# The mixer's loops in a two-block network: fill slices in one piece, weight parts in quarters, v transposes and the fifth loop moved

## The chip, the cores and the metric

The kernel runs on one core of one Trainium2 chip. Its time is the device time of one execution in microseconds (us); the median of three runs of the kernel before is 1939.12 (1939.05 to 1939.25). One program computes everything: TensorE (PE), VectorE (DVE), ScalarE (ACT), GpSimd (POOL) and SyncE (SP) each run their own queue in order and wait for one another by semaphores.

## The reference, cut to what matters

The input is 512 tokens of 1024 features. A first block is a token mixer and a gated feed-forward network with a short convolution. The second block has two layers, each with three attention branches. The change touches the token mixer alone:

```python
p = einsum('btd,de->bte', xn, w_in)            # 14 panels of weights
gB, gC, hA = split(p[..., :3 * CONV_DIM], 3)
y_a = gC * causal_dwconv(gB * hA, conv_a_w)
r, k, v, wd, ad, gd = split(shifted(p[..., 3 * CONV_DIM:]))
for each token:                                # _wkv7, state S of 64 x 64 for each of 8 heads
    sa = S @ (-kk_t)
    S = S * w_t + sa (kk_t * a_t)^T + v_t k_t^T
    y_t = S @ r_t
y_b = (group_norm(y) + bonus) * gate
out = concat(y_a, y_b) @ w_out
```

Everything is in float32. Each large product is made as three products of rounded parts: high x high, high x low and low x high.

## The kernel before

**Recurrence.** The tokens are taken in 4 tiles of 128 (TT), each of two chunks of 64. For a tile, `scores_0` makes the masked product of the two key forms. The inverse of a triangular 64 x 64 matrix for each head and chunk then comes from 6 levels (LEVELS). A level is: `level` on PE (L954, from the second level on also a transposition, L958), the masked step `T` on DVE (L1844), from the second level on the copy `inverse_t` on ACT (L1403), `update` on PE (L971), and the add into the inverse on DVE (L1853), which the next `level` waits for. These are groups of 32 small matmuls on quarters of the array. `whole_inverse` transposes the result.

**Five loops.** Loop c makes the inverse of tile c and, beside it, the state work of tile c - 1: `turn_bk`, `scores_1`, `scores_23` (L932; DVE masks them, L1829 and L1837), `kav` (L995, two ACT copies, L1419), and for each of the two chunks `state_rhs` (L1007), `state_sa` (L1043) and `state_out` (L1058, L1067, L1075); `values` (L1025, L1028) stands once for a tile. So there is a fifth loop (c = 4) with no inverse. This text calls c = 0 the first loop.

**Fill.** Between the small groups PE makes slices of the projection panels 9 to 13, which feed the convolution branch and the gate: a slice is one of 8 k blocks of one half panel, three matmuls of 128x512 (L596). `filler` deals out 80 slices: two ahead of the first level, then in each level two between `level` and `update` and one behind `update`. In the fifth loop, 24 slices of the output product (three matmuls of 128x256) take their place.

**Weights.** A panel arrives by DMA in `raw`. ACT rounds it to `wh` (`split_hi`, L352) once the panel two before it is used up, DVE makes `wl` as the difference (`split_lo_half`, L384, two halves), and PE waits for both. There are two buffers of each. SP loads panel p when `wl` of panel p - 2 is made.

**Other work on the queues.** DVE: `conv_in` (L1695), three `tap`s, `conv_out`, `bonus_gated` (L1728), the state's adds, and the parts of the group norm of a tile (`y_centred` after the `y_mean` product L831, `y_weighed`, `y_var`, `y_rstd` with a reciprocal, `y_mixed` after the `y_spread` product). ACT: squares and roots of the norm, the copies of the state work, `gates_scaled`. The order on each queue is written out by hand in four functions, `tensor`, `scalar`, `vector` and `sync`, and no planner changes it. The v transposes (`turn_v`, 16 of 128x128, L586) and their four copies on ACT (`v_tokens`, L1331) stand ahead of the loops; the first `scores_0` (L910) waits for the last copy.

**Output.** After the loops the output product runs by token tile t and column quarter i (panels 14 to 17). The products (2, t) and (3, t) wait for the low parts of panels 16 and 17, made by `split_lo_halves` (L374) and `split_lo`.

## Time and profile before

| | us |
|---|---|
| median of three runs | 1939.12 |
| profiled execution, its own time | 1943.69 |
| its span, first to last instruction | 1942.0 |
| v transposes, from their start to the first scores | 3.26 |
| first loop | 30.72 |
| loops two, three, four | 39.42, 41.27, 40.75 |
| fifth loop, from its first transposition to the mean of the last tile | 30.80 |
| from there to the first product that uses panel 16 | 17.93 |

The page gives the busy time of each engine; a window gives the same for a stretch with the granted clock of TensorE; a list of waits gives idle time by who waited and who released; the timeline gives single instructions. The ends of matmuls are modelled, so the pace of TensorE is read from start to start.

### The profile page before, as it was taken

What the parts mean: (1) busy time and instruction counts of PE and PEld (TensorE: products, weight loads), DVE (VectorE), ACT (ScalarE), POOL (GpSimd) and SP (SyncE); (2) the same over time, 40 slices, a digit from 0 to 9 for tenths busy, and PEclk for the clock granted to TensorE, in tenths of its full rate; (3) what the DMA queues carried; (4) which work ended last, traced back from release to release, by engine and by line L of the source; (5) the groups of instructions that cost most, each with busy time, mean ns of one, the idle gap of its engine ahead of it and who ended that gap; (6) DMA issues with size and microseconds to landing.
All of it is one profiled execution on the core that took longest, in us unless ns stands there. A gap on an engine that the chain in (4) does not pass through costs nothing.

```text
span 1942.0 us, 30355 instructions
## 1 busy us (share of the span) xinstructions
PE 1901.2 (98%) x12689; PEld 1538.2 (79%) x12689; DVE 1158.0 (60%) x1714; ACT 749.6 (39%) x1082; POOL 32.1 (2%) x72
## 2 busy tenths in 40 slices
PE   7999999999999999999999999999999999999999
PEld 5677778888888888787777788888787777778887
DVE  5854554677675344456687855545446678764534
ACT  5623333422222344533444434334533445334421
POOL 3000000020000000000000000000000000000000
PEclk9999999999999999999999999999999999999999
DMA  4311113233333323222123222232322222222232
GB/s 151 95 55 46 36 35 114 62 109 92 104 88 107 109 76 109 65 88 83 48 71 104 87 66 76 76 130 66 100 75 78 85 66 76 87 87 66 66 109 87
DMA packets 166021, 161.65 MB, mean 83 GB/s; under 512 B 13877, under 2 KB 150363, under 8 KB 165883
## 3 DMA queue, kind: packets, MB, share of 16 engines
q1 hardware_dynamic: 165184, 158.99, 26.0%
q8 instruction: 99, 1.62, 0.4%
q10 hardware_dynamic: 698, 0.71, 0.1%
q14 instruction: 40, 0.32, 0.1%
HBM read 157.59 MB, written 2.10 MB: 82 GB/s over the span
## 4 chain that ended last, share of the span: by engine, by line
PE 77%; DVE 2%; ACT 1%; issue 0%; ACTq 0%; DVEq 0%
PE psum L596 63%; PE psum L2036 5%; PE psum L2531 2%; PE psum L2508 1%; PE psum L586 1%; PE psum L2488 1%; PE psum L2516 1%; DVE w_lo L393 1%; PE psum L523 1%; ACT w_hi L352 0%; PE psum L532 0%; PE psum L2612 0%; DVE h_lo L457 0%; DVE ffn_normed L470 0%; PE psum L2597 0%; DVE w_lo L374 0%
## 5 line engine op out<-in xcount | busy, mean ns | idle before, releaser
L596 PE MATMUL psum<-h_hi,w_hi 128*128 128x512 f32 (+1 forms) x1568 | 611.7, 390 | 10.7 <-DVE h_lo L457 6.1
L596 PE MATMUL psum<-h_lo,w_hi 128*128 128x512 f32 (+1 forms) x1568 | 595.5, 380 | 0.0
L596 PE MATMUL psum<-h_hi,w_lo 128*128 128x512 f32 (+1 forms) x1568 | 595.4, 380 | 0.0
L393 DVE TENSOR_TENSOR w_lo<-w_raw,w_hi 128x2048 fp32r<-128x2048 f32 (+2 forms) x143 | 299.4, 2094 | 284.1 <-ACT w_hi L352 281.6
L352 ACT ACTIVATE w_hi<-w_raw 128x2048 fp32r<-128x2048 f32 (+1 forms) x148 | 260.8, 1762 | 369.8 <-PE psum L596 299.1
L596 PEld LDWEIGHTS psum<-h_hi,w_hi 128*128 128x128 f32 x1568 | 295.3, 188 | 88.1 <-issue 15.7
L596 PEld LDWEIGHTS psum<-h_hi,w_lo 128*128 128x128 f32 x1568 | 295.5, 188 | 56.3
L596 PEld LDWEIGHTS psum<-h_lo,w_hi 128*128 128x128 f32 x1568 | 295.7, 189 | 51.9 <-issue 0.2
L596 PE MATMUL psum<-w_hi,h_hi 128*128 128x512 f32 (+1 forms) x512 | 183.9, 359 | 2.6 <-DVE w_lo L393 1.7
L596 PE MATMUL psum<-w_lo,h_hi 128*128 128x512 f32 (+1 forms) x512 | 179.8, 351 | 0.0
L596 PE MATMUL psum<-w_hi,h_lo 128*128 128x512 f32 (+1 forms) x512 | 179.7, 351 | 0.0
L596 PEld LDWEIGHTS psum<-w_hi,h_hi 128*128 128x128 f32 x512 | 97.6, 191 | 30.0 <-issue 11.0
L596 PEld LDWEIGHTS psum<-w_hi,h_lo 128*128 128x128 f32 x512 | 97.7, 191 | 12.9
L596 PEld LDWEIGHTS psum<-w_lo,h_hi 128*128 128x128 f32 x512 | 97.7, 191 | 11.9 <-issue 0.2
L596 PE MATMUL psum<-y_hi,w_hi 128*128 128x512 f32 x192 | 80.1, 417 | 0.0
L596 PE MATMUL psum<-y_hi,w_lo 128*128 128x512 f32 x192 | 75.2, 392 | 0.0
L596 PE MATMUL psum<-y_lo,w_hi 128*128 128x512 f32 x192 | 75.1, 391 | 0.0
L2126 DVE TENSOR_SCALAR ffn_conv<-psum,ffn_cols 128x512 f32<-128x512 f32 x44 | 35.6, 810 | 63.3 <-PE psum L596 62.2
L2814 ACT ACTIVATE squares<-psum 128x512 f32<-128x512 f32 x48 | 28.7, 598 | 110.6 <-PE psum L596 110.2
L2036 PE MATMUL psum<-w_hi,ffn_hi 128*128 128x512 f32 x176 | 68.7, 390 | 0.5 <-DVE ffn_conv L2132 0.5
L2036 PE MATMUL psum<-w_lo,ffn_hi 128*128 128x512 f32 x176 | 68.5, 389 | 0.0
L2036 PE MATMUL psum<-w_hi,ffn_lo 128*128 128x512 f32 x176 | 68.5, 389 | 0.0
(370 smaller groups left out, 2185.5 us busy)
## 6 DMA issues: line engine op xcount, KB each, us to landing
w_raw<-in_w_in_dram SPq DMA_DIRECT2D x170, 512.0 KB, 4.4
w_raw<-in_w_up_dram SPq DMA_DIRECT2D x44, 512.0 KB, 5.1
w_raw<-in_w_out_dram SPq DMA_DIRECT2D x24, 512.0 KB, 4.5
w_raw<-in_w_br_dram SPq DMA_DIRECT2D x48, 256.0 KB, 3.0
w_raw<-in_w_down_dram SPq DMA_DIRECT2D x22, 512.0 KB, 4.3
x_first<-in_x_dram SPq DMA_DIRECT2D x4, 512.0 KB, 5.1
x_tokens<-in_x_dram SPq DMA_DIRECT2D x4, 512.0 KB, 5.1
out_dram<-x_tokens SPq DMA_DIRECT2D x4, 512.0 KB, 2.6
```

What stands on the lines that cost most here:

```text
L352: act.eng.activation(m.wh[:, g % 2, 0:n], m.raw[:, g % 2, 0:n], ACT.Copy).then_inc(act.done, 1)
L393: eng.eng.tensor_tensor(m.wl[:, g % 2, 0:n], m.raw[:, g % 2, 0:n], m.wh[:, g % 2, 0:n].bitcast(F32), ALU.subtract).then_inc(eng.done, 1)
L523: last = pe.eng.matmul(out[q, :], m.ind[:, kind, q], x[:, j, :], start=begin, stop=end, skip_group_check=True)
L586: last = pe.eng.transpose(m.PS[0:n, bank, rows * i:rows * i + rows], b, m.ident[at:at + rows, at:at + rows])
L596: last = pe.eng.matmul(out, a(k), b(k), start=(opens and k == 0 and i == 0), stop=(k == kt - 1 and i == 2), skip_group_check=ks is not None)
L2036: last = pe.matmul(PS[:, 2 * t + n, :], g[:, kk % 2, k, tt], w[:, k, cc], start=(kk == 0 and k == 0 and i == 0), stop=(kk == DN - 1 and k ...
L2126: dve.tensor_scalar(c, z, tap[2], bias, ALU.mult, ALU.add).then_inc(dve_done, 1)
L2488: pe.matmul(o[:, 0:vis], m.Q[r, h // 2, P * i:P * i + P], m.ikf[r, 0:vis], start=True, stop=True).then_inc(pe_done, 1)
L2508: last = pe.matmul(o[:, 0:vis], m.Q[r, h, P * i:P * i + P], m.K[r, h, 0:vis], start=True, stop=True)
L2516: pe.matmul(o[:, 0:vis], m.Q[:, h, P * i:P * i + P], m.K[:, h, 0:vis], start=True, stop=True).then_inc(pe_done, 1)
L2531: last = pe.matmul(o[:, 0:P], m.V[:, k, P * h:P * h + P], m.PT[:, u % 2, P * k:P * k + P], start=(k == 0), stop=(k == i))
L2814: act.activation(m.sq3[:, 2 * (r % 2) + i, :], PS[:, bank(p, i), :], ACT.Tanh, scale=0.5).then_inc(act_done, 1)
```

## The change

The change reorders the mixer's queues and cuts two kinds of work differently. The arithmetic stays the same.

- `joined(c, l)`: in the first two levels of loop 0 and the first four of loops 1 to 3, the three fill slices of a level stand in one piece between `level` and `update`. The state work of these levels moves behind `update`. `kav` waits for the first of the two masked scores alone.
- Low parts are made in quarters, at places given by `LO_AT`, between the mask and the add on DVE (`ready`); what needs the slices' products (`from_products`) stands ahead of the add in joined levels and behind it in others. High parts are made in halves on ACT (`hi_half`), a level apart. `bonus_gated` and the scaling of the gates are spread over levels by `BONUS_AT` and `SCALE_AT`.
- The v transposes and copies stand in the first two levels of the first loop.
- The fifth loop is written out: `scores_23` first, in banks 4 and 5, then `turn_bk` and `scores_1` in bank 2; the 24 output slices come in six groups of four, in another order.
- The first product with panel 16 starts on the first half of its low part.

In the long functions only the lines that are added and those that stay are shown; the lines that they replace stand in the kernel above.

```diff
+def split_hi_half(act, m, g, n, half):
+    c = slice(n // 2 * half, n // 2 * (half + 1))
+    act.wait_ge(*act.point(("w raw", g)))
+    act.wait_ge(act.sems["pe"], act.at(("w used", g - 2)))
+    act.wait_ge(act.done, act.so_far())
+    act.eng.activation(m.wh[:, g % 2, c], m.raw[:, g % 2, c], ACT.Copy).then_inc(act.done, 1)
+    act.counted(("w hi", g) if half else ("w hi half", g))
...
-def split_lo_half(eng, m, g, n, half):
-    c = slice(n // 2 * half, n // 2 * (half + 1))
+def split_lo_part(eng, m, g, n, part, parts):
+    c = slice(n // parts * part, n // parts * (part + 1))
     eng.wait_ge(eng.done, eng.so_far())
-    eng.wait_ge(eng.sems["act"], eng.at(("w hi", g)))
+    eng.wait_ge(eng.sems["act"], eng.at(("w hi half", g) if 2 * part < parts else ("w hi", g)))
     eng.eng.tensor_tensor(m.wl[:, g % 2, c], m.raw[:, g % 2, c], m.wh[:, g % 2, c].bitcast(F32),
                           ALU.subtract).then_inc(eng.done, 1)
-    eng.counted(("w lo", g) if half else ("w lo half", g))
+    eng.counted(("w lo", g) if part == parts - 1 else ("w lo part", g, part))
...
+def joined(c, l):
+    return l < 2 if c == 0 else l < 4
...
-            slots[c, l, 0], slots[c, l, 1] = 2, 1
+            slots[c, l, 0], slots[c, l, 1] = (3, 0) if joined(c, l) else (2, 1)
...
+LO_AT = {9: ((0, 3), (0, 5), (1, 1), (1, 4)), 10: ((0, 3), (1, 1), (1, 4), (1, 6)), 11: ((0, 4), (0, 6), (0, 7), (1, 1)),
+         12: ((0, 2), (0, 6), (1, 3), (1, 5)), 13: ((0, 3), (1, 0), (1, 1), (1, 4))}
+BONUS_AT = {(0, 0): 0, (0, 5): 1, (1, 1): 2, (1, 4): 3}
+SCALE_AT = {(0, 3): 0, (1, 0): 1, (1, 2): 2, (1, 5): 3}
...
-    for c, offsets in ((2, (2, 5, 6, 8, 11)), (3, (6, 9, 10, 13, 16))):
+    for c, offsets in ((2, (2, 5, 6, 8, 11)), (3, (6, 9, 10, 14, 17))):
...
         def fill(slot):
-            for p, i, k in fill_steps.get(slot, ()):
+            steps = fill_steps.get(slot, ())
+            normed = [(*y_steps[p, i, k], 1 - bank(p, i)) for p, i, k in steps if (p, i, k) in y_steps]
+            for what, t, b in normed:
+                if what == "spread":
+                    y_spread(t, b)
+            for p, i, k in steps:
                 if k == 0:
...
+                if what == "mean":
+                    y_mean(t, b)
+                if what == "sums":
+                    y_sums(t, b)
...
-        early = [(i, t, k) for i, t in ((0, 0), (1, 0), (0, 1)) for k in range(KT)]
-        def last_fill(l):
-            n = len(early) // (LEVELS - 2)
-            for i, t, k in early[n * (l - 2):n * (l - 1)] if l > 1 else ():
+        early = [(0, 0, k) for k in range(JT)] + [(0, 1, k) for k in range(JT)]
+        early += [(0, 0, k) for k in range(JT, KT)] + [(0, 1, k) for k in range(JT, KT)]
+        early += [(1, 0, k) for k in range(KT)]
+        def out_steps(first, end):
+            for i, t, k in early[first:end]:
                 out_step(i, t, k)
...
         def kav(c):
-            E.wait_ge(dve_done, E.at(("SC23", c)))
+            E.wait_ge(dve_done, E.at(("SC2", c)))
...
+        for c in range(TT):
             s = 2 * c - 2
+            scores_0(c)
             if c > 0:
                 turn_bk(c - 1)
             fill(c)
             if c > 0:
+                scores_1(c - 1, 4)
             for l in range(LEVELS):
+                level(c, l)
+                if c > 0 and l == 4:
+                    state_rhs(s + 1)
+                if c > 0 and l == 5:
+                    state_sa(s + 1)
                 fill((c, l, 0))
+                update(c, l)
+                if c == 0 and l < 2:
+                    turn_v(2 * l)
+                    turn_v(2 * l + 1)
+                if c > 0 and l == 0:
+                    scores_23(c - 1, 6)
+                if c > 0 and l == 1:
+                    kav(c - 1)
+                    state_rhs(s)
                 if c > 0 and l == 2:
+                    values(c - 1, 0)
+                    state_sa(s)
                     values(c - 1, 1)
+                if c > 0 and l == 3:
+                    state_out(s)
                 fill((c, l, 1))
             if c > 0:
                 state_out(s + 1)
+            whole_inverse(c)
+        c, s = TT - 1, 2 * TT - 2
+        scores_23(c, 4)
+        turn_bk(c)
+        scores_1(c, 2)
+        y_mean(TT - 2, 1)
+        state_rhs(s)
+        kav(c)
+        values(c, 0)
+        out_steps(0, 4)
+        state_sa(s)
+        values(c, 1)
+        out_steps(4, 8)
+        y_sums(TT - 2, 3)
+        state_out(s)
+        out_steps(8, 12)
+        y_spread(TT - 2, 1)
+        state_rhs(s + 1)
+        out_steps(12, 16)
+        state_sa(s + 1)
+        out_steps(16, 20)
+        state_out(s + 1)
+        out_steps(20, 24)
         y_mean(TT - 1, 7)
...
         for i, t in ((2, 0), (2, 1), (3, 0), (3, 1), (2, 2), (2, 3), (3, 2), (3, 3)):
-            E.wait_ge(*E.point(("w lo", NPROJ + i)))
             if i == 2:
                 banks.use(2 * t + 1, seam.key("post out", t))
-            out_part(i, t, range(KT)).then_inc(pe_done, 1)
+            if (i, t) == (2, 0):
+                E.wait_ge(*E.point(("w lo half", NPROJ + i)))
+                out_part(i, t, range(KT // 2))
+            E.wait_ge(*E.point(("w lo", NPROJ + i)))
+            out_part(i, t, range(KT // 2 if (i, t) == (2, 0) else 0, KT)).then_inc(pe_done, 1)
...
         E.wait_ge(act_done, E.so_far())
         E.wait_ge(pool_done, E.at(("masks", 1, LEVELS - 1)))
-        for c in range(TT):
+        def v_tokens(c):
...
+        def slots(c, l):
+            return [x for i in range(2) for x in fill_steps[c, l, i]]
+        def panel_ends(c, l):
+            return [p for p, i, k in slots(c, l) if k == KT - 1 and i == 1 and p < NPROJ - 1]
+        def gates_out(c, l):
+            for p, i, k in slots(c, l):
                 if k == KT - 1 and p == 11:
                     E.wait_ge(dve_done, E.at(("ya", i)))
                     evacuate(p, i)
+        def y_parts(c, l):
+            for x in slots(c, l):
...
                 bk_tokens(c - 1)
+            ended = []
             for l in range(LEVELS):
+                if l > 0:
                     inverse_t(c, l)
+                for p in ended:
+                    hi_half(p + 2, 1)
+                ended = panel_ends(c, l)
+                if c == 0 and l < 2:
+                    v_tokens(2 * l)
+                    v_tokens(2 * l + 1)
+                if l == 3:
+                    for p in ended:
+                        hi_half(p + 2, 0)
                 if c > 0 and l == 1:
                     kav(c - 1)
                 if c > 0 and l in (2, 5):
                     state_sa(s + l // 4)
                 if c > 0 and l == 3:
                     y_state(s)
+                if l != 3:
+                    for p in ended:
+                        hi_half(p + 2, 0)
+                y_parts(c, l)
+                gates_out(c, l)
+                if (c, l) == (0, 2):
+                    spread_rows()
+                if (c, l) in SCALE_AT:
+                    gate_scaled(SCALE_AT[c, l])
             if c > 0:
                 y_state(s + 1)
+            if c == TT - 1:
+                mix_hi(0, 0, 0, 2)
+            whole_inverse(c)
             if c < TT - 1:
                 whole_ident(c + 1)
+        c, s = TT - 1, 2 * TT - 2
+        bk_tokens(c)
+        hi_half(NPROJ + 1, 0)
+        y_square(TT - 2)
+        kav(c)
+        mix_hi(1, 1, 0, 2)
+        hi_half(NPROJ + 1, 1)
+        state_sa(s)
+        y_root(TT - 2)
+        y_state(s)
+        mix_hi(0, 1, 2, 4)
+        mix_hi(1, 2, 2, 3)
...
+        def ready(slots):
+            for p, i, k in slots:
+                before = (p, 0) if i else (p - 1, 1)
+                if before[0] in (9, 12) and k in (2, 4, 6):
+                    tap(*before, 3 - k // 2)
+                if (i, k) in LO_AT[p]:
+                    split_lo_part(E, m, p + 1, KT * PW, LO_AT[p].index((i, k)), 4)
+                what, t = y_steps.get((p, i, k), (None, 0))
+                if what == "sums":
+                    y_weighed(t)
+                if what == "split":
+                    y_rstd(t)
+        def from_products(slots):
+            for p, i, k in slots:
                 if k == KT - 1 and p in (9, 12):
                     conv_in(p, i)
                 if k == KT - 1 and p in (10, 13):
                     conv_out(p, i)
+            for p, i, k in slots:
                 what, t = y_steps.get((p, i, k), (None, 0))
+                if what == "mean":
+                    y_centred(t)
+                if what == "root":
+                    y_var(t)
+                if what == "spread":
...
+                steps = fill_steps[c, l, 0] + fill_steps[c, l, 1]
+                level(c, l)
+                ready(steps)
+                if joined(c, l):
+                    from_products(steps)
+                update(c, l)
+                if c > 0 and l == 0:
+                    scores_23(c - 1, 6)
+                if c > 0 and l in (1, 4):
+                    state_rhs(s + l // 4)
+                if c > 0 and l == 3:
+                    state_next(s)
+                    y_out(s)
+                if not joined(c, l):
+                    from_products(steps)
+                if (c, l) in BONUS_AT:
+                    bonus_gated(BONUS_AT[c, l])
             if c > 0:
+                state_next(s + 1)
+                y_out(s + 1)
+        c, s = TT - 1, 2 * TT - 2
+        scores_23(c, 4)
+        scores_1(c, 2)
+        y_centred(TT - 2)
+        mix_lo(0, 0, 0, 2, (0,))
+        y_weighed(TT - 2)
+        state_rhs(s)
+        mix_lo(1, 1, 0, 2, (0, 1))
+        for half in range(2):
+            split_lo_part(E, m, NPROJ + 1, KT * PW, half, 2)
+        y_var(TT - 2)
+        state_next(s)
+        y_rstd(TT - 2)
+        y_out(s)
+        y_scaled(TT - 2)
+        state_rhs(s + 1)
+        y_mix(TT - 2)
+        mix_lo(0, 1, 2, 4, (1,))
+        mix_lo(1, 2, 2, 3, (2,))
+        y_out(s + 1)
         y_centred(TT - 1)
         y_weighed(TT - 1)
```

## Rows read from the trace of the kernel before

**Rows 1.** The page: the span, and busy time of each engine.

```profile
span 1942.0 us, 30355 instructions
PE 1901.2 (98%) x12689; PEld 1538.2 (79%) x12689; DVE 1158.0 (60%) x1714; ACT 749.6 (39%) x1082; POOL 32.1 (2%) x72
```

**Rows 2.** Windows: the v transposes, first loop, fifth loop, output stage.

```profile
core 0: us, PE busy (x) PEld busy (x) DVE busy (x) ACT busy (x) POOL busy (x), PEclk, DMA share, GB/s
129.63:132.89 3.26, 1.91 (x18) 1.68 (x16) 1.07 (x3) 2.42 (x5) 0.00 (x0) 1.00 0.00 0
132.89:163.61 30.72, 29.23 (x667) 22.00 (x669) 15.10 (x25) 5.51 (x7) 0.00 (x0) 0.94 0.12 37
285.05:315.85 30.80, 25.69 (x388) 22.95 (x386) 16.32 (x23) 12.93 (x19) 0.00 (x0) 0.89 0.11 36
315.85:333.78 17.93, 17.01 (x139) 15.98 (x139) 7.68 (x11) 4.49 (x6) 0.00 (x0) 1.00 0.39 139
```

**Rows 3.** TensorE's waits, 131 to 334 us: total, times, longest.

```profile
PE psum L954 <- DVE inverse L1853: 2.5, 3, 1.1
PE psum L971 <- ACT inverse_t L1403: 2.5, 2, 1.5
PE psum L596 <- DVE w_lo L393: 1.7, 1, 1.7
PE psum L995 <- DVE scores L1837: 1.6, 2, 1.5
PE psum L910 <- ACT v_tokens L1331: 1.3, 1, 1.3
PE psum L831 <- DVE y_feats L1883: 1.0, 1, 1.0
PE psum L596 <- DVE w_lo L374: 0.9, 1, 0.9
PE psum L1025 <- ACT chunk_kav L1419: 0.7, 1, 0.7
PE psum L932 <- ACT b_k_tokens L1396: 0.2, 1, 0.2
```

**Rows 4.** Windows at the low clock in the mixer's loops, columns as rows 2.

```profile
149.03:152.45 3.42, 3.42 (x61) 2.92 (x54) 3.10 (x4) 0.60 (x1) 0.00 (x0) 0.50 0.26 69
302.63:309.46 6.83, 6.83 (x44) 6.59 (x44) 3.94 (x7) 0.63 (x1) 0.00 (x0) 0.50 0.48 154
```

**Rows 5.** Timeline of two levels in the first loop: start, length, engine, line.

```profile
137.29 0.67 PE L971 MATMUL psum<-inverse_step,chunk_ident 64*64 64x32 f32 x32
137.88 0.50 PE L596 MATMUL psum<-h_hi,w_hi 128*128 128x512 f32 x1
138.08 0.43 DVE L1853 TENSOR_TENSOR inverse<-psum,inverse 128x256 f32<-128x256 f32 x1 [1.75 <-PE psum L971]
...
138.78 0.67 PE L954 MATMUL psum<-inverse,scores_a_b 64*64 64x32 f32 x32
139.26 0.67 PE L958 MATMUL psum<-chunk_ident,inverse 64*64 64x64 f32 x32
139.87 0.50 PE L596 MATMUL psum<-h_hi,w_hi 128*128 128x512 f32 x1
...
140.62 0.60 ACT L1403 ACTIVATE inverse_t<-psum 128x512 f32<-128x512 f32 x1 [7.12 <-DVE inverse_step L1844]
...
141.47 0.67 PE L971 MATMUL psum<-inverse_step,inverse_t 64*64 64x32 f32 x32
```

**Rows 6.** Groups by line and form, loops: busy, mean ns, idle before.

```profile
L384 DVE TENSOR_TENSOR w_lo<-w_raw,w_hi 128x1024 fp32r<-128x1024 f32 x10 | 12.3, 1225 | 0.3
L1728 DVE SCALAR_TENSOR_TENSOR bonus_v<-bonus_v,param_cols,gates 128x512 f32<-128x512 f32 x4 | 3.0, 752 | 0.1
L1695 DVE TENSOR_TENSOR conv_in<-psum,conv_gate 128x512 f32<-128x512 f32 x4 | 2.8, 692 | 3.3 <-PE psum L596 3.3
...
L1419 ACT ACTIVATE chunk_kav<-psum 64x512 f32<-64x512 f32 x8 | 4.7, 592 | 2.4 <-PE psum L995 2.0
```

More of the change, by code:

```diff
@@ L70, in __init__ @@
         self.w = sum(c[2] for c in pieces)
-SHARED = ("seam", "w raw", "w hi half", "w hi", "w lo half", "w lo", "w used")
+SHARED = ("seam", "w raw", "w hi half", "w hi", "w lo half", "w lo part", "w lo", "w used")
 class Steps:
@@ L1436, in y_state, with hi_half @@
                 E.counted(("y state", s, e))
+        def hi_half(p, part):
+            split_hi_half(E, m, p, KT * PW, part)
+        E.wait_ge(dve_done, E.at(("q", NZ - 1)))
         whole_ident(0)
-        for c in range(TT + 1):
+        for c in range(TT):
             s = 2 * c - 2
@@ L1882, in state_out @@
             E.wait_ge(pe_done, E.at(("y mm", s)))
-            dve.tensor_tensor(y, PS[:, 7, w].rearrange("p (j n) -> p j n", j=JT), y, ALU.add).then_inc(dve_done, 1)
+            dve.tensor_tensor(y, PS[:, 7, part(s)].rearrange("p (j n) -> p j n", j=JT), y, ALU.add).then_inc(dve_done, 1)
             E.counted(("y", s))
         E.wait_ge(pool_done, E.at(("masks", 1, LEVELS - 1)))
-        for c in range(TT + 1):
+        for c in range(TT):
             s = 2 * c - 2
-            if c < TT:
-                scores_0(c)
-            fill_tail(c)
-            if c == TT:
-                y_centred(TT - 2)
+            scores_0(c)
+            ready(fill_steps[c])
+            from_products(fill_steps[c])
```

185 lines of the change are left out of this document (45 added, 140 removed).

## The prediction

> **What bounds the kernel now.** The page comes first: TensorE is busy for 98% of the span [rows 1], so only what its own queue loses can shorten the kernel. DVE and ACT matter where they make it wait. The change touches the mixer alone, so I next read the windows of its loops [rows 2]: the v transposes take 3.26 us, the first loop 30.72, the fifth 30.80, the output stage up to the second half's first product 17.93. The reader is to see how much thinner TensorE is in the fifth loop (25.69 busy of 30.80) and that the granted clock is below 1 in the first and fifth loops. The list of waits [rows 3] gives TensorE's idle time from 131 to 334 us: 2.5 + 2.5 + 1.7 + 1.6 + 1.3 + 1.0 + 0.9 + 0.7 + 0.2 = 12.4 us. The windows at the low clock [rows 4] give 3.42 us (just behind a 1.5 us wait of the first loop) and 6.83 us (behind the 1.7 us wait of the fifth) at 0.50, that is 1.2 instead of 2.4 GHz. PE is busy throughout both, so half of each was lost: 1.7 and 3.4 us. The rest is pace: how the blocks of the queue follow each other [rows 5]. The sum is made on the profiled execution (span 1942.0, own time 1943.69) and carried one to one to the median of 1939.12, since what is around the mixer is not edited.
>
> **1. v transposes moved (before the loops to the first loop).** TensorE waits 1.3 us there for the fourth v copy [rows 3] because the first scores stand behind all copies. After the change scores_0 waits for the bonus products' readers only, which DVE finishes while the last product runs (0.69 us each); I take 0.2 us for it. The 16 transposes still run, 8 behind each of the first two updates, where a one-slice fill block stood; the 2 slices move into the block ahead. What is saved beside the wait is the fixed cost of two fill blocks. That cost comes from rows 5: the six-matmul block takes 141.47 - 139.87 = 1.60 us, the three-matmul block 138.78 - 137.88 = 0.90. So a slice is 0.70 and a block costs 0.20 on top. Two blocks: 0.4. Sum: 1.3 + 0.4 + 0.2 (short gaps around the wait) - 0.2 = **1.7 us**. What ACT now does in the loop (four copies of 0.6, the size of that in rows 5) has over 3 us a level in which ACT is idle (7.12 us before the first copy of the inverse [rows 5]). It costs nothing.
>
> **2. Stall and low clock in the first loop.** DVE has a conv product 0.69, half a low part 1.23 and a bonus 0.75 [rows 6] between one add into the inverse and the next level's mask. Together 2.67, where a level and its latency leave 1.6. The mask is late, then ACT's copy (DVE releases it), then the update: 1.5 us of the 2.5 us in the L971 row [rows 3]. In the new order the quarter parts (1.225 / 2 = 0.61 each) stand between mask and add. With two slices that gap is from just before 140.62 to 142.26 (the next add comes 0.79 behind the update's start, as at 137.29 and 138.08 [rows 5]), so 1.6 us; with three slices 2.3. The fullest two-slice slot of this loop holds a tap (no more than the bonus, 0.75) and a quarter, 1.36. It fits. After the add stands at most one operation of 0.75. I take the 1.5 as gone and with it the cause of the low clock behind it, 1.7: **3.2 us**. If the cover fails, both come back.
>
> **3. Slices in one piece, loops 2 to 4.** In 12 slots (l = 0 to 3) one of two fill blocks goes. Besides its 0.20, the change from small to large matmuls goes: L971 followed by a large one takes 137.88 - 137.29 = 0.59, L954 followed by small ones 139.26 - 138.78 = 0.48. So 0.31 to 0.32 a slot, 12 x 0.32 = **3.8 us**. This needs the next level not to wait for the add. The add ends 138.51 - 137.29 = 1.22 behind the update's first matmul, and TensorE needs at most 0.25 to see it (the copy that ends at 141.22 is used at 141.47): 1.35 to 1.47. What stands between is update 0.60 and scores_23, about 0.85 (32 matmuls of twice the columns of L954's 0.48): 1.45. So the cover just holds at l = 0, amply at l = 1 to 3 (kav and rhs, values and sa, state_out, each 1.4 or more).
>
> The Trainium skill says otherwise of pace: in "TensorE: Matmul & The Clock Gate", section Back-to-back issue gap, a matmul's step is its columns plus a few ns, with no term for a neighbour of another shape. By that rule this item is nil and the sum 3.8 less; rows 5 disagree: six matmuls take 1.60, three take 0.90 and not 0.80.
>
> **4. Waits of DVE and ACT in loops 2 to 4.** Of the 12.4 us, those of L954 (2.5), the other 1.0 of L971 and 0.2 of L995 are here: 3.7. In each of them a half part of 1.23 [rows 6] stands before the add or before the mask. Another 0.6 I add for delays too short for the list (modelled ends cover them). Quarters of 0.61 under a gap of 1.6 or 2.3 remove these. New ones, from walking DVE's and ACT's queues slot by slot: third loop, level 2, ACT does the kav copies (2 x 0.59 [rows 6]), a high half (half of what a whole takes, near 1.0), a root and an evacuation ahead of the inverse's copy: 0.3 late. In the fourth loop's level 4 the reciprocal and a quarter leave nothing spare: 0.1. Behind the y mean, and behind scores_23, 0.1 each. Together 0.8, between 0 and 3. Net **3.5 us**.
>
> **5. Fifth loop.** From 30.80 [rows 2] I take the waits of this stretch, 1.7 + 1.5 (the long one of L995) + 1.0 + 0.7 + 0.2 = 5.1, and the 3.4 of the low clock: 22.3 of work. New waits: y(5) now stands behind y_scaled and mix on DVE (2 x 0.69), of which scores_23, moved ahead of the transposes, covers 0.85: 0.5. And kav's copies on ACT stand behind the transposed b/k copies, a high half and y_square, which itself waits for the centring on DVE. I walk ACT as 2 x 0.6 + 1.0 + a wait + 0.6 + 2 x 0.6; TensorE finishes kav 5.1 us into the stage, and both copies are there at 6.7. values(0) waits **1.6 us**. The w lo 15 halves are done before the (1,0) slices, so the old 1.7 goes. 22.3 + 2.1 = 24.4: 6.4 less. But 0.5 and 1.6 close together look like what came before both low stretches of rows 4, so I keep one stretch of 3.41 at half clock: 1.7. Net **4.7 us** (6.4 without it, 3.0 with two). Nothing queues behind DVE's new wait for the rstd spread but rhs(7), covered by four out slices.
>
> **6. Output stage.** The first product of the second half waits 0.9 for the low part of panel 16 [rows 3], with the short gap 1.0. It may now start on the first half, which is finished 1.2 us earlier, and its four slices (12 matmuls of half the columns of those that take 0.70 / 3 each, so 1.4 us) outlast the rest. **1.0 us**. SyncE's loads (each waits for a low part that now ends earlier or at most a slot later) have tens of us before their use; POOL is not passed.
>
> **Sum:** 1.7 + 3.2 + 3.8 + 3.5 + 4.7 + 1.0 = 17.9. 1939.12 - 17.9 = **1921.2**.
>
> **Rivals.** (a) *The clock stays low more often.* The gaps are as in item 5, and the first loop is full of small matmuls. Two more stretches of 3.41 at half clock: 17.9 - 3.4, 1924.6. For it: it followed 1.5 and 1.7 us waits. Against: it did not follow the 1.47 us wait of the fifth loop or the 1.3 us at the start. The Trainium skill ("TensorE: Matmul & The Clock Gate", What's actually happening) has the chip's activity check run freely, not from the kernel's start; then a low stretch would come and go between runs. The three times differ by 0.2 us, which speaks for fixed places. (b) *No low stretch and no new waits.* 17.9 + 1.7 + 2.0: 1917.5. (c) *The wait for the add takes the place of the removed block.* The margin at l = 0 is nothing, and any DVE operation in front of the add shows directly. If all 14 joined slots lose 0.4: 5.6, 1926.8. (d) *The pieces pace as before* (item 3 is nil; the change does not do what it says): 1925.0. (e) *Slower.* One mechanism: `ready` puts 20 low quarters in front of the add, and each waits for a high half that ACT makes behind the inverse's copy. If the high half comes late, the add, the next level and ACT's next copy are late too, and the queue is in lockstep. It decides when a quarter holds the add by over 0.9 us: 20 x 1.0 = 20 us, 1941.2. Against: each high half is issued a level (over 4 us) before its quarter.
>
> **Chances.** Forecast 0.55, (a) 0.13, (b) 0.12, (c) 0.10, (d) 0.06, (e) 0.04. The 8-in-10 range takes in (b) and (a), and most of (c): 1916.5 to 1927.0. A measurement of this kernel can tell about 0.2%, 3.9 us, from no change; (a) to (d) are all beyond it. Faster 0.95, same 0.02, slower 0.03.
>
> **What would show it.** Item 1: first scores near 129.8, fourth v copy inside the loop. Item 2: no wait of L971 over 0.3 us before 165, clock 1.00. Item 3: 9-matmul blocks of 2.3 us, L954 right behind L932 and L1007. Item 4: no wait of TensorE for DVE over 0.5 us up to the fifth loop. Item 5: one wait of values(0) for ACT's kav copies, 1 to 2 us; y mean of the last tile 24 to 26 us behind the fourth loop's end. Item 6: no wait at the second half. Wrong if DVE's adds come late at l = 0, or if low clock shows at other places.

## The result, and the profile after

The changed kernel takes 1928.2 us (median of four executions, 1927.01 to 1929.26), the kernel before 1939.2 beside it (1939.05 to 1942.99). The ratio is 0.9938, with a 95% interval of 0.9926 to 0.9949: faster by 0.6%, 11.0 us. Forecast were 17.9 us and 1921.2, with a range of 1916.5 to 1927.0. The direction was right, the time lies 7.0 us above the forecast and 1.2 above the range.

The page of the changed kernel, profiled execution of 1927.01 us; these lines answer to [rows 1], and the last one is the DMA queue that carries instructions (packets, MB, share):

```profile
span 1925.3 us, 30380 instructions
PE 1891.2 (98%) x12689; PEld 1533.5 (80%) x12689; DVE 1159.2 (60%) x1725; ACT 750.9 (39%) x1088; POOL 32.0 (2%) x72
...
q8 instruction: 99, 1.62, 0.4%
```

TensorE executes the same number of instructions as before. Its windows in the changed kernel, to be held against [rows 2]: the first loop, the fifth loop from its transpositions to the last y mean, and the output stage:

```profile
core 0: us, PE busy (x) PEld busy (x) DVE busy (x) ACT busy (x) POOL busy (x), PEclk, DMA share, GB/s
129.24:160.51 31.27, 30.23 (x717) 23.18 (x717) 15.57 (x28) 10.45 (x19) 0.00 (x0) 1.00 0.12 37
278.25:301.86 23.61, 21.98 (x358) 19.43 (x356) 16.74 (x24) 11.87 (x19) 0.00 (x0) 1.00 0.15 47
301.86:318.54 16.68, 16.68 (x141) 15.86 (x140) 6.66 (x11) 3.70 (x5) 0.00 (x0) 1.00 0.37 137
```

The first loop now holds the v transposes and still needs 31.27, where these and the loop took 3.26 + 30.72; the window after even ends later in the program, at the first b/k transposition, 0.67 behind the first scores of the second loop, where that of [rows 2] ends. The granted clock is 1.00 in all three. TensorE's waits from 125 to 319 us (who waited, who released: total, times, longest), against [rows 3]:

```profile
PE psum L985 <- issue: 2.9, 5, 1.0
PE psum L1054 <- ACT chunk_kav L1471: 1.5, 1, 1.5
PE psum L981 <- issue: 1.1, 2, 0.7
PE psum L998 <- DVE norm_rows_hi L1833: 0.5, 1, 0.5
```

Of the 12.4 us of waits for DVE and ACT, 2.0 are left, and both were forecast (L1054 is values(0), L998 the update). The releaser of the second is named by the time alone: an update needs DVE's masked step and ACT's copy of the inverse (L1455), and the copy ends at 215.90, 0.14 before the update at 216.04. But seven waits of 4.0 us in all have appeared whose releaser is "issue": TensorE waited for nothing that the profile shows. L981 and L985 are the level's product and transposition (L954 and L958 before), L937 the first scores, L617 the fill slices.

### The profile page after: what moved, and what is told of

It reads as the page before. It is cut to its first block, busy times and chain, and to the rows that moved or that the text cites. A ratio compares the mean times of both kernels' runs of the same rounds, so it can differ in the third digit from the quotient of the medians.

```text
span 1925.3 us, 30380 instructions
## 1 busy us (share of the span) xinstructions
PE 1891.2 (98%) x12689; PEld 1533.5 (80%) x12689; DVE 1159.2 (60%) x1725; ACT 750.9 (39%) x1088; POOL 32.0 (2%) x72
## 3 DMA queue, kind: packets, MB, share of 16 engines
q8 instruction: 99, 1.62, 0.4%
## 4 chain that ended last, share of the span: by engine, by line
PE 78%; DVE 2%; ACT 1%; issue 0%; ACTq 0%; DVEq 0%
PE psum L617 64%; PE psum L2128 6%; PE psum L2623 2%; PE psum L2600 1%; PE psum L607 1%; PE psum L2580 1%; PE psum L2608 1%; PE psum L533 1%; DVE w_lo L403 1%; PE psum L542 0%; ACT w_hi L352 0%; PE psum L2704 0%; DVE h_lo L467 0%; PE psum L2689 0%; DVE w_lo L384 0%; PE psum L2657 0%
## 5 line engine op out<-in xcount | busy, mean ns | idle before, releaser
L617 PE MATMUL psum<-h_hi,w_hi 128*128 128x512 f32 (+1 forms) x1568 | 608.2, 388 | 10.9 <-DVE h_lo L467 6.3
L617 PE MATMUL psum<-h_lo,w_hi 128*128 128x512 f32 (+1 forms) x1568 | 594.4, 379 | 0.0
L617 PE MATMUL psum<-h_hi,w_lo 128*128 128x512 f32 (+1 forms) x1568 | 594.4, 379 | 0.0
L403 DVE TENSOR_TENSOR w_lo<-w_raw,w_hi 128x2048 fp32r<-128x2048 f32 (+1 forms) x142 | 297.1, 2092 | 283.0 <-ACT w_hi L352 280.5
L352 ACT ACTIVATE w_hi<-w_raw 128x2048 fp32r<-128x2048 f32 (+1 forms) x142 | 249.3, 1756 | 366.2 <-PE psum L617 295.8
L617 PEld LDWEIGHTS psum<-h_hi,w_hi 128*128 128x128 f32 x1568 | 294.4, 188 | 88.6 <-issue 16.3
L617 PEld LDWEIGHTS psum<-h_hi,w_lo 128*128 128x128 f32 x1568 | 294.5, 188 | 55.8
L617 PEld LDWEIGHTS psum<-h_lo,w_hi 128*128 128x128 f32 x1568 | 294.7, 188 | 52.4
L617 PE MATMUL psum<-w_hi,h_hi 128*128 128x512 f32 (+1 forms) x512 | 183.0, 357 | 0.0
L617 PE MATMUL psum<-w_lo,h_hi 128*128 128x512 f32 (+1 forms) x512 | 179.0, 350 | 0.0
L617 PE MATMUL psum<-w_hi,h_lo 128*128 128x512 f32 (+1 forms) x512 | 178.9, 349 | 0.0
L617 PEld LDWEIGHTS psum<-w_hi,h_hi 128*128 128x128 f32 x512 | 96.8, 189 | 27.1 <-issue 11.0
L617 PEld LDWEIGHTS psum<-w_hi,h_lo 128*128 128x128 f32 x512 | 96.8, 189 | 12.8
L617 PEld LDWEIGHTS psum<-w_lo,h_hi 128*128 128x128 f32 x512 | 96.9, 189 | 11.9 <-issue 0.2
L617 PE MATMUL psum<-y_hi,w_hi 128*128 128x512 f32 x192 | 80.1, 417 | 0.0
L617 PE MATMUL psum<-y_hi,w_lo 128*128 128x512 f32 x192 | 75.2, 392 | 0.0
L617 PE MATMUL psum<-y_lo,w_hi 128*128 128x512 f32 x192 | 75.1, 391 | 0.0
```

The costliest lines, as they stand in the source:

```text
L352: act.eng.activation(m.wh[:, g % 2, 0:n], m.raw[:, g % 2, 0:n], ACT.Copy).then_inc(act.done, 1)
L403: eng.eng.tensor_tensor(m.wl[:, g % 2, 0:n], m.raw[:, g % 2, 0:n], m.wh[:, g % 2, 0:n].bitcast(F32), ALU.subtract).then_inc(eng.done, 1)
L617: last = pe.eng.matmul(out, a(k), b(k), start=(opens and k == 0 and i == 0), stop=(k == kt - 1 and i == 2), skip_group_check=ks is not None)
```

## Where the new idle time is

The timeline of TensorE in the changed kernel, first at the end of the first loop (start, length, line, count), then in the fourth:

```profile
153.60 0.67 PE L981 MATMUL psum<-inverse,scores_a_b 64*64 64x32 f32 x32
154.09 0.67 PE L985 MATMUL psum<-chunk_ident,inverse 64*64 64x64 f32 x31
155.74 0.21 PE L985 MATMUL psum<-chunk_ident,inverse 64*64 64x64 f32 x1 [0.99 <-issue]
155.89 0.50 PE L617 MATMUL psum<-h_hi,w_hi 128*128 128x512 f32 x1
...
245.04 0.60 PE L981 MATMUL psum<-inverse,scores_a_b 64*64 64x32 f32 x27
245.99 0.25 PE L981 MATMUL psum<-inverse,scores_a_b 64*64 64x32 f32 x3 [0.34 <-issue]
```

Such a stop lies in the middle of a group. The trace shows no wait of the instruction behind it, which has the same operands' tiles as its neighbours in the group, so no engine's result is missing. In the stretch from 153 to 157 us the list of DMA queues of the changed kernel shows one packet of the instruction queue:

```profile
q8 instruction: 1, 0.02, 1.8%
```

In the trace its record begins at 153.28 and ends at 154.40, and TensorE goes on at 155.74. The page has 99 such packets, 1.62 MB, so 16 KB each. TensorE has 12689 matmuls and as many weight loads; shared out over 99 packets that is about 256 records each. Counting TensorE's records in order (matmuls, weight loads and the 130 records of its sequencer), I found every stop of the mixer at a count that leaves 193 when divided by 256, and each ends 1.3 to 1.5 us behind the end of a packet's record:

```
changed kernel, first profile (start to start over the gap; time since the packet's end)
record 2241 at 155.74 us  1.21  1.34      record 6849 at 245.98 us  0.56  1.47
record 3521 at 179.93 us  0.76  1.40      record 7617 at 259.40 us  0.74  1.51
record 3777 at 185.76 us  0.91  1.51      record 7873 at 264.78 us  0.42  1.27
record 5569 at 219.99 us  0.83  1.42      sum 5.4
```

This says that TensorE waits there for its own instructions, and the borders without a stop say it too: with packet and border matched in order, no record at such a border starts sooner than 1.26 us behind the end of its packet, at none of the 98 or 99 borders of any of the 14 profiles of this case. A 128x512 matmul takes 0.23 us from start to start, so 256 records of fill (128 matmuls) feed it for 29 us; in a group such as L981 128 matmuls take 2 us. The packet ahead of a stop begins 127 to 205 records before the border, no later than many of the others (half of those in the mixer begin 194 records ahead or less). 194 records are 97 matmuls: small ones at 0.015 us use them up in 1.5 us, while the packet takes 0.9 to 1.4 us (once 2.2) and TensorE goes on 1.3 to 1.5 us behind it.

The kernel before breaks the small groups with fill blocks: its longest run of small matmuls without one has 112 of them in a level and 120 where a loop turns; in the levels in one piece of the changed kernel's loops 2 to 4 it is 128 in the first, then 144 to 152, 176 to 184, and 160. Six of the seven stops lie in such runs. The first and longest does not: at record 2241 the run has 64, no more than the kernel before has there. Its packet begins late, 127 records before the border. The kernel before had one such stop of 0.34 us in the execution of the forecast's rows.

## Experiments

**The kernel before, unchanged, once more.**

> The kernel before once more, unchanged, to see where a second execution has its low-clock stretches. Theory 1 (low stretches belong to an execution, not to a place of the kernel): the profiled span and each run's granted clock go together, every 3.41 us at 0.50 costs about 1.7 us, and the stretches at 149 and 303 us are missing or elsewhere in this profile; runs near 1939.1 have a mean clock of 0.997 or 0.998, the profiled one of 1943.69 had 0.995. Rival (they belong to the stalls before them): low stretches at 149 and 303 us again, and the span is 1942 again.

Measured: 1940.79 (1938.1 to 1944.6), ratio 1.0 [0.9991, 1.001]. Its profiled execution took 1939.47. Windows of this second execution: the two stretches of [rows 4], then its fifth loop:

```profile
149.03:152.45 3.42, 3.42 (x89) 2.68 (x82) 2.92 (x5) 0.00 (x0) 0.00 (x0) 1.00 0.02 5
302.63:309.46 6.83, 6.83 (x75) 6.49 (x74) 4.91 (x8) 1.14 (x2) 0.00 (x0) 1.00 0.47 156
...
285.49:313.27 27.78, 22.68 (x388) 20.04 (x386) 16.32 (x23) 12.91 (x19) 0.00 (x0) 1.00 0.12 40
```

Both are at 1.00 here, although the waits in front of them are the same. The mixer, from the first bonus product to the first product of panel 16, takes 203.63 us instead of 207.58. So these two stretches do not come in every execution. 47 timed executions of this kernel agree: nine with a mean clock of 0.995 took 1943.8 on average, fifteen with 0.999 took 1939.6. The forecast's profile was one at 0.995. It does not follow that places mean nothing: all 14 profiles of this case have a stretch between 726 and 746 us, and that of the kernel before with padding (below) has one at 303 again.

The second execution also shows a wait that the first had covered. In front of the update behind the stretch at 149 us, ACT makes its copy, and TensorE waits:

```profile
152.96 0.60 ACT L1403 ACTIVATE inverse_t<-psum 128x512 f32<-128x512 f32 x1 [4.51 <-DVE inverse_step L1844]
153.70 0.67 PE L971 MATMUL psum<-inverse_step,inverse_t 64*64 64x32 f32 x32 [0.87 <-DVE conv_gate L1707]
```

(The profile names the DVE operation that ended last before the update; what the update needs is the copy, ended at 153.56, 0.14 before it.) In the forecast's execution this update starts without a wait: TensorE, at half clock, came later. So the stretch at 149 cost little there: from the first bonus product to the first transposition of the second loop that execution took 38.07 us, this one 37.55.

**The changed kernel once more.**

> The changed kernel once more. Theory 1: runs spread from about 1926 to 1931 with clocks from 0.999 down to 0.996, 1.7 us for each low stretch, at places that differ from the first profile's 728.6 us. Theory 2 (PE waits for its own instruction packets): the same seven gaps without a releaser inside groups of small matmuls, each ending 1.3 to 1.5 us behind the landing of a 16384-byte packet of the instruction queue, 3.7 us idle in all. Rival of theory 2 (the gaps are disturbances of one execution): they are at other places.

Measured: 1928.86 (1928.14 to 1929.48), ratio 0.9939 [0.9926, 0.9951]. Six stops, at records 2241, 3521, 3777, 5569, 7617 and 7873, together 4.4: the same records within 1 us of time, without the one at 6849. They belong to the kernel, though not each of them comes in every execution. Of the low stretches here, at 352, 362 and 731 us, the first profile has only the last (at 729).

**First scores made three, four and five times.** The copies only repeat a product into the same place, and add 128, 192 and 256 records ahead of everything else in the mixer. A stop that hangs on the count moves, one that hangs on the work stays.

```
 def scores_0(c):
-            for j in range(JT):
+            for j in list(range(JT)) * (3 if c == 0 else 1):      # 4, 5 in the others
```

> The changed kernel with the first tile's first scores made three times over (128 more TensorE records, same result). Theory 2: a packet holds 256 records, so all later packet borders move by half a packet: the gaps at the old seven places vanish and gaps appear, if at all, half a packet further on; the count may be from 3 to 8. The added groups themselves cost 0.9 us. Rival (a gap belongs to the group of small matmuls in which it stands): the same seven gaps in the same groups, time plus 0.9 us.

Measured: 1925.51 (1923.81 to 1927.1), ratio 0.9922 [0.9908, 0.9935]. The timeline of this kernel at the place of the first stop, and its waits:

```profile
153.23 0.67 PE L981 MATMUL psum<-inverse,scores_a_b 64*64 64x32 f32 x32
153.72 0.67 PE L985 MATMUL psum<-chunk_ident,inverse 64*64 64x64 f32 x32
154.32 0.50 PE L617 MATMUL psum<-h_hi,w_hi 128*128 128x512 f32 x1
...
PE psum L1054 <- ACT chunk_kav L1471: 1.5, 1, 1.5
PE psum L1054 <- issue: 1.2, 1, 1.2
PE psum L998 <- DVE norm_rows_hi L1833: 0.5, 1, 0.5
```

With 0.93 us of work more, the median is 3.4 us below that of the changed kernel beside it, and the mixer takes 189.56 us against its 192.03 (192.98 in the first profile). The stops fall from 4.4 to 1.9: those left are at records 4033 (0.54 behind the first matmul of a fill block, where 0.34 is usual) and 5569 (1.39). Stops and padding explain 1.6 of the 2.5 us by which the mixer is shorter; the rest, 0.9, is no more than the two profiles of the changed kernel differ by.

> The changed kernel with the first scores made five times over (256 more TensorE records). Theory 2: borders fall where they fell in the changed kernel, so the same seven gaps in the same groups; time plus 1.9 us, less what moves with the low clock. Rival (a gap belongs to a moment or to other DMA traffic): the places change.

Measured: 1929.57 (1928.59 to 1930.01), ratio 0.9942 [0.9927, 0.9957]. A whole packet more, and the old stops are back, each a packet later in the count and at the same place of the work: 2497, 3777, 4033, 5825, 7873 and 8129 stand for 2241, 3521, 3777, 5569, 7617 and 7873. The mixer takes 193.78, close to the 192.03 of the changed kernel beside it and 1.9 of padding. The median is 0.7 above that kernel's, less than the 1.9, within what the executions spread by. The waits of this kernel:

```profile
PE psum L985 <- issue: 2.8, 5, 0.9
PE psum L1054 <- ACT chunk_kav L1471: 1.5, 1, 1.5
PE psum L998 <- DVE norm_rows_hi L1833: 0.5, 1, 0.5
PE psum L981 <- issue: 0.2, 1, 0.2
```

> The changed kernel with the first scores made four times over (192 more TensorE records, 1.4 us of work, same result). Theory 2: borders at another phase, so the gaps are elsewhere again; counting runs of small matmuls ahead of each border gives 2 to 3 us of gaps instead of 5.4, so about -1 us against the changed kernel. Rival (more records, more time): +1.4 us and gaps as before.

Measured: 1927.01 (1925.85 to 1927.58), ratio 0.9926 [0.9909, 0.9942]; two stops, 1.3 together, and a mixer of 190.02. It has fewer stops than the version with three times the scores, but 0.5 more of padding.

**The same padding in the kernel before.** The edit is that of the first of the three.

> The kernel before with the same 128 records added to its first scores. Theory 2: its fill blocks stand close enough that packets are always there in time (no gap at a border over 0.35 us in either profile of it), so the shift gives nothing and costs its 0.9 us. Rival (the phase of the records helps any kernel, or the gain of 3.3 us in the changed kernel has nothing to do with its long runs): 2 us or more faster than the kernel before.

Measured: 1941.8 (1940.93 to 1945.31), ratio 1.0006 [0.9996, 1.0015]; no stop. The median of the kernel before beside it is 1940.99. Here the padding buys nothing: the gain above is not one of the padding itself.

**Twelve fill blocks put back**, a second one in each of the first four levels of loops two to four:

```
 def joined(c, l):
-    return l < 2 if c == 0 else l < 4
+    return c == 0 and l < 2
```

> The changed kernel with the fill slices of loops two to four in two pieces again (2 ahead of the update, 1 behind it); the rest of the new order stays. Theory 2 (PE waits for its instruction packets where small matmuls run on without a fill block): the second piece breaks every run of small matmuls, the gaps at packet borders in loops two to four fall from 4.2 us to under 1, and 12 blocks more cost 12 x 0.32 = 3.8 us: about 0 +- 1 us against the changed kernel. Rival (joining gives its full 3.8 us and the gaps have another cause): the gaps stay and the time is 3.8 us longer.

Measured: 1928.31 (1927.03 to 1929.91), ratio 0.9932 [0.9917, 0.9947]. The waits of this kernel:

```profile
PE psum L1054 <- ACT chunk_kav L1471: 1.5, 1, 1.5
PE psum L985 <- issue: 0.7, 1, 0.7
PE psum L998 <- DVE norm_rows_hi L1833: 0.2, 1, 0.2
```

One stop of 0.9 is left of seven, at record 2241, in the first loop that this edit doesn't touch. Twelve blocks more cost 3.8 by the forecast's own price, the stops give 3.5 to 4.5 back: the time is that of the changed kernel, and so is the mixer with 192.13. Joining the slices in loops 2 to 4 earned nothing in the end, not because the pace was misjudged, but because what it saved was lost to the packets.

**Six of the twelve**, in the third and fourth level of these loops:

```
 def joined(c, l):
-    return l < 2 if c == 0 else l < 4
+    return l < 2
```

> The changed kernel with slices in one piece in the first two levels of each loop alone. Theory 2: of the gaps at packet borders those at levels 2 and 3 (records 3521, 3777, 5569, 7617, 7873: 3.3 us over their normal pace in the two profiles) go, 6 blocks more cost 6 x 0.32 = 1.9 us: about 1.4 us faster than the changed kernel. Rival (joining is worth its 0.32 a level wherever it stands and the gaps move instead of going): 0 to 2 us longer.

Measured: 1928.8 (1928.15 to 1930.23), ratio 0.9941 [0.9928, 0.9955]. The waits of this kernel:

```profile
PE psum L1054 <- ACT chunk_kav L1471: 1.5, 1, 1.5
PE psum L998 <- DVE norm_rows_hi L1833: 1.2, 1, 1.2
PE psum L985 <- issue: 0.9, 1, 0.9
PE psum L998 <- DVE w_lo L394: 0.6, 1, 0.6
```

The stops fell nearly as expected, to 1.4: 2241 and, of 0.35, 4801, which had shown no stop. But six blocks more cost 1.9, and the two rows of L998 add 1.3 to the 0.5 of before. In both the update starts 0.14 behind ACT's copy of the inverse (ended at 177.25 and 217.40): with one slice less ahead of it, TensorE comes to the update sooner and waits longer for the same copy. The gain that I expected did not come.

**v transposes ahead of the loops again**, slices as in the changed kernel. ACT's queue is turned to match, and its wait for DVE ahead of the loops goes:

```
+        for c in range(TT):
+            turn_v(c)
...
-                if c == 0 and l < 2:
-                    turn_v(2 * l)
-                    turn_v(2 * l + 1)
```

> The changed kernel with the 16 v transposes and their four copies ahead of the loops again; the fill slices of the first two levels stay in one piece, so nothing stands between update and level there. Theory (item 1 and the cover of item 3): the first scores wait about 0.9 us for the third copy (bank), and each of the two levels waits 0.6 to 0.8 us for DVE's add, so the time from the bonus products to the first b/k transposition grows by 2.0 to 2.6 us against the changed kernel. Rival (the transposes were no cover, the add was never late): only the 0.9 us. TensorE's record count is the same, borders of packets fall 64 records earlier in the queue's work for the first levels and as before later.

Measured: 1931.54 (1930.03 to 1932.6), ratio 0.9954 [0.994, 0.9967]. The waits of this kernel:

```profile
PE psum L985 <- issue: 2.2, 4, 0.8
PE psum L981 <- DVE inverse L1933: 1.7, 2, 1.1
PE psum L1054 <- ACT chunk_kav L1470: 1.7, 1, 1.7
PE psum L937 <- ACT v_tokens L1373: 0.8, 1, 0.8
PE psum L998 <- DVE norm_rows_hi L1830: 0.5, 1, 0.5
PE psum L981 <- issue: 0.4, 1, 0.4
```

The start and first loop take 36.85 instead of 34.9: 2.0 us. Moved forward again, the transposes cost their wait for a v copy (0.8), and they leave the first loop bare: with nothing between update and next level there, the add comes late twice (1.7). In the changed kernel they are the cover of the slots that have no fill block behind the update.

**Two quarters of the low part back to back**, so that in effect halves are made, at two slots in each panel.

```
-LO_AT = {9: ((0, 3), (0, 5), (1, 1), (1, 4)), ...}
+LO_AT = {(0, 7): (0, 1), (1, 2): (2, 3)}
```

> The changed kernel with the four quarters of each low part made two at a time at the two places where the kernel before had its halves, still between mask and add. Theory (item 4: a half of 1.23 us in front of the add or mask is what made TensorE wait): waits of TensorE for the add come back in levels with two slices, 1 to 3 of them of 0.3 to 1.0 us in loops two to four, time 1 to 2.5 us longer. Rival (the larger window of joined levels is enough): no wait of TensorE for DVE's add over 0.3 us, time as the changed kernel.

Measured: 1929.32 (1928.23 to 1929.79), ratio 0.9944 [0.9929, 0.9959]. The waits of this kernel:

```profile
PE psum L984 <- issue: 2.3, 5, 0.8
PE psum L1053 <- ACT chunk_kav L1470: 1.5, 1, 1.5
PE psum L980 <- DVE inverse L1935: 1.1, 2, 0.6
PE psum L980 <- issue: 0.7, 1, 0.7
PE psum L997 <- DVE norm_rows_hi L1832: 0.5, 1, 0.5
```

Only two adds come late, by 1.1 together. The mixer takes 193.16, where the changed kernel takes 192.03 and 192.98. With the slices in one piece the gap that DVE has is longer, and halves nearly fit; by these two waits the quarters are worth some 1 us, which neither the mixer nor the median can show. The stops are six here, with one at record 1985 that no other profile has.

**The y mean of the fifth loop behind kav**, with ACT's and DVE's queues turned to match (kav's copies ahead of y_square, the mix and state_rhs ahead of the centring):

```
-        y_mean(TT - 2, 1)
         ...kav...
+        y_mean(TT - 2, 1)
```

> The changed kernel with the mean product of the third tile moved behind kav in the fifth loop (and its square, centring and weighing one place later on ACT and DVE). Theory (TensorE waits 1.5 us for the two kav copies because nothing stands between kav and values): the product covers 0.9 us of them, the wait at the first values product falls from 1.5 to about 0.5 us, time -1.0 us. Rival (ACT is late from its own queue): wait and time unchanged. The record count and the packet borders stay, so the gaps at borders stay too.

Measured: 1928.12 (1926.2 to 1929.47), ratio 0.993 [0.9915, 0.9945]. The waits of this kernel:

```profile
PE psum L985 <- issue: 2.9, 5, 0.8
PE psum L998 <- DVE norm_rows_hi L1833: 0.5, 1, 0.5
PE psum L1054 <- ACT chunk_kav L1471: 0.4, 1, 0.4
PE psum L981 <- issue: 0.2, 1, 0.2
```

The wait of values(0) falls from 1.5 to 0.4, and the mixer to 190.92, 1.1 to 2.1 less. The median can't show this little: 1928.1 against 1928.2 and 1928.9.

**Both together**, three times the first scores and the later y mean:

> The later mean product of the fifth loop and the 128 added records together, a candidate for the best version. If both effects are independent: 3.3 us from the phase and 1.0 us from the mean product, 1924.4 +- 1 us, mixer from bonus to the first product with panel 16 188.5 us. If they share a cause, 1925.5.

Measured: 1926.27 (1923.87 to 1928.3), ratio 0.9927 [0.9914, 0.9939]. The waits of this kernel:

```profile
PE psum L1054 <- issue: 0.9, 1, 0.9
PE psum L1054 <- ACT chunk_kav L1471: 0.4, 1, 0.4
PE psum L998 <- DVE norm_rows_hi L1833: 0.2, 1, 0.2
```

The mixer was as expected, 188.6 (forecast 188.5). The whole was not: 1.9 above the forecast. In the profiled execution a stretch at the low clock, at 350 us, costs part of it; the rest is not explained. Its best is 1923.87. This version and the one with the padding alone have lower medians than both kernels, by 0.7 to 0.8% against the kernel before; they can't be told apart. That they beat the changed kernel too rests on medians 1.9 to 3.4 us lower, while the intervals of the ratios overlap.

## Why the prediction was off

The mixer in stages, from the first bonus product, all at full clock (before: second profile; after: first; the scores_23 product of 0.84 us is counted with the fifth loop in both):

```
                            before  after   gain   + stops   forecast at full clock
start and first loop         37.54  34.95    2.6    3.8      3.2
loops 2 to 4                120.38 116.90    3.5    7.7      7.3
fifth loop                   27.78  24.45    3.3    3.3      3.0
output, to panel 16          17.93  16.68    1.25   1.25     1.0
sum                         203.63 192.98   10.65  16.1     14.5
```

Two steps failed: low clock was counted that the median had not paid, 3.4 us, and stops of TensorE for its instructions, 5.4 us in this profile (4.4 in the second), were not counted at all. Together 8.8 of the 17.9; the rest of the sum came out 1.6 us above its 14.5.

**The low clock (items 2 and 5).** The sum counted 1.7 + 1.7 = 3.4 us for stretches at 1.2 GHz that the change would remove with the waits in front of them. They belonged to one execution: in the second one the waits are there and the stretches are not. The step that failed is "carried one to one to the median". The profiled execution's own time of 1943.69 was 4.6 above a median of 1939.12, and its mixer took 3.95 more than that of the second; a gain read from it that the three timed executions had not paid could not be had in the median. Rival (a) took the low clock for the kernel's too, only more of it. That three times lay within 0.2 us was no evidence of fixed places. The Trainium skill ("TensorE: Matmul & The Clock Gate", section What's actually happening) has the chip's check of activity run freely and not from the kernel's start. The stretches at 149 and 303 us, which come and go between executions, agree with it; that between 726 and 746 us, which every profile has, it does not explain.

Item 2 also gave its stretch the wrong size. At 149 us the low clock cost some 0.5 us and not 1.7, because it covered the wait of 0.87 for ACT's copy that the second execution shows. The change removes that wait as well, which no term counted. It is of the size by which the first row of the table exceeds its forecast, 3.8 against 3.2.

Whether the change makes low stretches rarer in the mixer is not settled. None of the eleven profiles of the changed kernel and its versions has one there; of the three of the kernel before, with and without padding, two have.

**TensorE's own instructions (item 3).** This is not in the forecast at all. The price of a block (0.32 each) held: the first one of nine matmuls runs from 132.05 to 134.31, 2.26 where 2.3 was forecast, and loops 2 to 4 give 7.7 with the stops added back. From the first transposition of the second loop to that of the fifth, the version with twelve blocks put back takes 117.16 us without a stop, the changed kernel (second profile) 116.92 with 3.3 us of stops: 3.5 for twelve blocks, 0.30 each. What came in place is 4.2 us of stops in these loops and 1.2 in the first. Of the rivals (c) came nearest in time (1926.8), but by another mechanism: no add of DVE held TensorE in the joined slots. Rival (d) would have left 12 x 0.32 in the pace, and its blocks would not take 2.26. I had compared block costs and never asked how long a run of small matmuls lasts. The stop in the first loop is no matter of that length, and no run here removes it except by shifting the records.

The other items:

- Item 1: the first scores start at 129.24, 3.68 behind the first bonus product, where 3.43 is what the products take in the kernel before: a wait of 0.25 (forecast 0.2). The version with the transposes ahead gives 2.0 for this item and its cover together.
- Item 2: no wait of L998 before 165; the 1.5 is gone, as forecast, and so is the 0.87.
- Item 4: one wait in the loops, 0.5 in the third, level 2, for ACT's copy of the inverse behind the kav copies, a high half, a root and an evacuation. That is where ACT was to be 0.3 late. The other new waits, of 0.1 each, are too short for the list; as they are named, all of them add up to 0.6 and not to the 0.8 of the sum. The low quarter takes more than half of a half part, the group of the changed kernel shows it (busy, mean ns):

```profile
L394 DVE TENSOR_TENSOR w_lo<-w_raw,w_hi 128x512 fp32r<-128x512 f32 x20 | 13.8, 692 | 0.7
```

  692 ns against the 0.61 of the forecast. The cover held nonetheless.
- Item 5: 24.45 us against 24.4, and the wait for kav's copies is 1.5 (forecast 1.6). The other wait of the sum, 0.5 behind DVE's y work, does not show, so that the total fits to 0.05 is in part luck:

```profile
284.17 0.24 PE L1054 MATMUL psum<-v_tokens,b_k_tokens 64*64 64x64 f32 x1 [1.47 <-ACT chunk_kav L1471]
```

- Item 6: 1.25 (forecast 1.0), no wait at the second half.
- Rival (b) added 2.0 for the new waits, where items 4 and 5 count 0.8 and 2.1; with 2.9 it would have been 1916.6 and not 1917.5.
- Rival (e) did not occur: no low quarter held an add.

What stays open: whether the place in the packet (a remainder of 193) comes from how far ahead TensorE asks for packets or from where its program starts; and what sets the moment at which a packet begins, since only its record is in the trace. That the length of the run of small matmuls decides in loops two to four rests on the versions with fewer joined slots and on the kernel before; no run here has varied the length of a run alone, and the stop at record 2241 comes in a run of 64.

## What to carry to other kernels

Before a sum is made on a profile, compare its own time and mean clock with the median: what a low stretch cost there belongs in the sum only if the timed executions paid it too, and a second profile of the same kernel settles it. When large matmuls between groups of small ones are merged or removed, count the instructions in the run that results and look for stops with "issue" as releaser, in the middle of a group; the small groups consume instructions some fifteen times as fast as the fill (29 us against 2 us a packet). A stop of this kind can be moved off by a few instructions placed earlier, and a shift by a whole packet of 256 records is the test that it was one.

## What the runs showed of the hardware

- TensorE can run out of instructions. The stops last 0.3 to 1.4 us each, begin at a fixed place of a packet of 256 records and end 1.3 to 1.6 us behind the end of the packet's record; in 14 profiles nothing ever passed that place sooner than 1.26 us behind it. The stops appeared in stretches of small products (64x32 or 64x64) at 0.015 to 0.02 us each; that at record 4033 of the padded kernel stands right behind such a stretch.
- A subtraction over 128x512 takes DVE 692 ns and one over 128x1024 1225 [rows 6]: two quarters cost 0.16 more than a half.
- The same program had low-clock stretches at 149, 303, 367 and 746 us in one execution and, apart from its end, only at 742 us in another. Executions of the kernel before with a mean clock of 0.995 to 0.999 lie between 1938.1 and 1944.6 us; that spread of 6.5 us is more than half of what this change is worth.
- A low-clock stretch can cost less than half its length. That at 149 us lasted 3.4 us and cost some 0.5, since TensorE would else have waited 0.87 for ACT.
